# Eight norms' roots taken with tokens on the partitions, and spread by a product with diagonals

## What is computed

```
def rms_norm(x, g):
    y = x * rsqrt(mean(x * x, axis=-1) + EPS)
    return y * g

def modulate(h, shift, scale):
    return h * (1.0 + scale) + shift

h = modulate(rms_norm(x, norm_g[layer, 0]), sh, sc)
x = x + 0.5 * (1.0 + g) * swiglu(h, w_in, w_out)
...
x = x + gate * _rmsnorm(merged @ w_out, g_post)
```

## Time and profile before

| | us |
|---|---|
| median of three runs | 1347.66 |
| profiled execution | 1349.85 |
| span of its instructions | 1348.1 |
| TensorE with work | 1275.7 |
| VectorE busy | 1079.7 |
| ScalarE busy | 633.5 |
| GpSimd busy | 184.8 |

### The profile page before, as it was taken

How to read it: one execution, slowest core, us unless ns; L and a number is a source line. 1 busy time by engine, 2 the same in 40 slices (tenths; PEclk the granted TensorE clock), 3 DMA queues, 4 the chain that set the end, 5 groups by cost and what they waited for, 6 DMA issues and landing times.

```text
span 1348.1 us, 26718 instructions
## 1 busy us (share of the span) xinstructions
PE 1275.7 (95%) x10588; PEld 1238.6 (92%) x10588; DVE 1079.7 (80%) x1692; ACT 633.5 (47%) x990; POOL 184.8 (14%) x205
## 2 busy tenths in 40 slices
PE   1899999899999999999999999999999898999996
PEld 1899999799999889999999999999998788999996
DVE  6898977898877868889888686999876786895574
ACT  3543444444334556544457543433455465355452
POOL 4498900000000000000001000000001220430000
PEclk9899999999999999999999999999999998999998
DMA  9999897399897369988843468996656486455551
GB/s 362 341 326 308 305 311 262 126 309 333 303 314 272 125 216 358 335 301 303 310 138 113 156 247 300 329 321 207 229 165 169 88 146 151 158 166 180 178 181 48
DMA packets 110893, 319.82 MB, mean 237 GB/s; under 512 B 24096, under 2 KB 35648, under 8 KB 110528
## 3 DMA queue, kind: packets, MB, share of 16 engines
q1 hardware_dynamic: 110784, 318.31, 70.7%
HBM read 313.26 MB, written 5.01 MB: 236 GB/s over the span
## 4 chain that ended last, share of the span: by engine, by line
PE 85%; DVE 7%; ACT 3%; DMA 3%; issue 2%; SPq 1%; DVEq 0%; ACTq 0%
PE tiles L375 17%; PE tiles L377 17%; PE tiles L376 17%; PE acc L375 8%; PE acc L376 8%; PE acc L377 8%; PE nrm L547 1%; ACT w_hi L363 1%; DMA cons<-in_cons 1%; DVE w_lo L367 1%; PE tiles L573 1%; PE acc L686 1%; PE tiles L575 1%; PE tiles L590 1%; DVE arena L1456 1%
## 5 line engine op out<-in xcount | busy, mean ns | idle before, releaser
L363 ACT CAST w_hi<-land 128x1024 fp32r<-128x1024 f32 x391 | 408.3, 1047 | 465.7 <-PE tiles L377 289.1
L367 DVE TENSOR_TENSOR w_lo<-land,w_hi 128x1024 fp32r<-128x1024 f32 x391 | 484.9, 1247 | 160.2 <-ACT w_hi L363 159.3
L375 PE MATMUL tiles<-x_hi,w_hi 128*128 128x256 f32 x1384 | 395.2, 286 | 8.1 <-ACT arena L1133 3.9
L376 PE MATMUL tiles<-x_lo,w_hi 128*128 128x256 f32 x1384 | 392.6, 284 | 0.0
L377 PE MATMUL tiles<-x_hi,w_lo 128*128 128x256 f32 x1384 | 392.6, 284 | 0.0
L375 PEld LDWEIGHTS tiles<-x_hi,w_hi 128*128 128x128 f32 x1384 | 266.5, 193 | 11.2 <-ACT arena L1133 4.4
L376 PEld LDWEIGHTS tiles<-x_lo,w_hi 128*128 128x128 f32 x1384 | 266.5, 193 | 0.1
L377 PEld LDWEIGHTS tiles<-x_hi,w_lo 128*128 128x128 f32 x1384 | 266.4, 193 | 0.0
L1411 DVE SCALAR_TENSOR_TENSOR arena<-arena 128x1024 f32<-128x1024 f32 x184 | 227.1, 1237 | 12.3 <-ACT arena L1156 8.8
L375 PE MATMUL acc<-h_hi,w_hi 128*128 128x256 f32 x704 | 199.4, 283 | 1.5 <-DVE h_lo L1430 1.5
L376 PE MATMUL acc<-h_lo,w_hi 128*128 128x256 f32 x704 | 199.2, 283 | 0.0
(11 more groups left out here) (342 smaller groups left out, 1634.8 us busy)
## 6 DMA issues: line engine op xcount, KB each, us to landing
land<-in_stream SPq DMA_DIRECT2D x391, 512.0 KB, 4.5
arena<-in_gstream SPq DMA_DIRECT2D x184, 512.0 KB, 6.4
w_dram<-arena SPq DMA_DIRECT2D x3, 512.0 KB, 6.4
arena<-w_dram SPq DMA_DIRECT2D x6, 256.0 KB, 9.3
arena<-in_c_rows SPq DMA_DIRECT2D x2, 512.0 KB, 6.4
x<-in_x_t SPq DMA_DIRECT2D x1, 1024.0 KB, 12.9
arena<-in_ssm_bn SPq DMA_DIRECT2D x1, 1024.0 KB, 7.6
u_dram<-arena SPq DMA_DIRECT2D x1, 1024.0 KB, 5.3
```

Of the source, the lines that this page charges most:

```text
L363: nc.scalar.copy(w_hi[:, u % RING], land[:, u % LAND]).then_inc(hi_done, 1)
L367: nc.vector.tensor_tensor(w_lo[:, u % RING], land[:, u % LAND], w_hi[:, u % RING].bitcast(F32), ALU.subtract).then_inc(lo_done, 1)
L375: nc.tensor.matmul(outs, lh, rh, start=first, stop=False, **kw)
L376: nc.tensor.matmul(outs, lh, rl, start=False, stop=False, **kw)
```

## The change

The sums of squares, the roots and the reciprocals of all eight norms are taken with tokens on the partitions. `sum_squares` uses each squared tile as the loaded operand, in two halves of 128 tokens, with one column of ones streaming (`token_sums`): sixteen products of one column instead of eight of 256, into the last two columns of the bank `nrm`. Sqrt and reciprocal then have 128x2 values (`token_root`). VectorE multiplies the identity matrix with each of the two columns, which gives two diagonal matrices side by side (`root_diag`, 128x256, in the place where `rx` was), and signals `diag_done`. TensorE multiplies a matrix of ones with them (`spread_roots`), which puts the reciprocal root of every token on all partitions, and `rx` is now the first half of the bank `nrm` in PSUM. VectorE waits for that (`spread`) before it takes the normalised tiles. `keep_busy(7)` becomes `keep_busy(2)`, `spread_roots`, `keep_busy(3)`; at norm 6 `keep_busy(3)` becomes `keep_busy(2)`, `spread_roots`, `keep_busy(1)`, ahead of the small products; at norm 4 the spread stands behind two thirds of the transposes. Since the bank is now read until the last normalised tile, TensorE waits for `t_done` instead of `rt_done` before it writes there again.

```
+        eps_root, token_root = sb("eps_root", [P, 1])[:], sb("token_root", [P, 2])[:]
...
-        rx = region(36, [T])
+        root_diag = region(36, [2, P])
...
+        rx, sums = nrm[:, 0:T], nrm[:, 510:512]
...
                 if n:
-                    pe.wait_ge(rt_done, n)
+                    pe.wait_ge(t_done, KT * (n if n < 4 else n + 1))
                 for k in range(KT):
                     pe.wait_ge(sq_done, KT * n + k + 1)
-                    m = nc.tensor.matmul(nrm[:, 0:T], ones, t_buf[:, k], start=(k == 0), stop=(k == KT - 1))
+                    m = token_sums(t_buf[:, k], k == 0, k == KT - 1)
                 m.then_inc(nrm_done, 1)
+
+            def token_sums(squares, start, stop):
+                for tt in range(2):
+                    m = nc.tensor.matmul(sums[:, tt:tt + 1], squares[:, tt * P:(tt + 1) * P], ones[:, 0:1],
+                                         start=(start and tt == 0), stop=stop, skip_group_check=True)
+                return m
+
+            def spread_roots(n):
+
+                pe.wait_ge(diag_done, n + 1)
+                nc.tensor.matmul(rx, ones, root_diag.rearrange("p a b -> p (a b)"), start=True,
+                                 stop=True).then_inc(rx_done, 1)
...
             sum_squares(0)
+            spread_roots(0)
...
             sum_squares(1)
-            keep_busy(7)
+            keep_busy(2)
+            spread_roots(1)
+            keep_busy(3)
...
             for c, bank in enumerate((tiles[:, 0], tiles[:, 1], av_bank)):
                 turn_keys(c + 1, bank)
+                if c == 1:
+                    spread_roots(4)
             keep_busy(2)
...
             sum_squares(6)
-            keep_busy(3)
+            keep_busy(2)
+            spread_roots(6)
+            keep_busy(1)
...
             pe.wait_ge(sq_sum, KT - 2)
-            nc.tensor.matmul(nrm[:, 0:T], ones, t_buf[:, 0], start=True, stop=False)
+            token_sums(t_buf[:, 0], True, False)
             pe.wait_ge(sq_done, KT * 8)
-            nc.tensor.matmul(nrm[:, 0:T], ones, t_buf[:, KT - 1], start=False, stop=True).then_inc(nrm_done, 1)
+            token_sums(t_buf[:, KT - 1], False, True).then_inc(nrm_done, 1)
+            spread_roots(7)
...
-                nc.scalar.activation(rx, nrm[:, 0:T], ACT.Sqrt, bias=con("eps", 1), scale=1.0 / D).then_inc(rt_done, 1)
+                nc.scalar.activation(token_root, sums, ACT.Sqrt, bias=con("eps", 1), scale=1.0 / D).then_inc(rt_done, 1)
...
             def root(n):
                 dve.wait_ge(rt_done, n + 1)
-                link(V.reciprocal(rx, rx))
+                link(V.reciprocal(token_root, token_root))
+                V.tensor_tensor(root_diag, ident.unsqueeze(1).to_broadcast([P, 2, P]),
+                                token_root.unsqueeze(2).to_broadcast([P, 2, P]), ALU.mult).then_inc(diag_done, 1)
+
+            def spread(n):
+                dve.wait_ge(rx_done, n + 1)
```

More of the change, by code:

```diff
@@ L167, in build_program @@
         mods = sb("mods", [P, N_MOD])
-        eps_root = sb("eps_root", [P, 1])[:]
+        eps_root, token_root = sb("eps_root", [P, 1])[:], sb("token_root", [P, 2])[:]
         att_s = sb("att_s", [P, 2, 16])
@@ L287, in build_program @@
         sq_done, nrm_done, rt_done = sem("sq_done"), sem("nrm_done"), sem("rt_done")
+        diag_done, rx_done = sem("diag_done"), sem("rx_done")
         t_done, xh_done, xl_done = sem("t_done"), sem("xh_done"), sem("xl_done")
@@ L756, in _ @@
             sum_squares(2)
-            keep_busy(7)
+            keep_busy(2)
+            spread_roots(2)
+            keep_busy(3)
             ffn(1, 2)
             sum_squares(3)
-            keep_busy(7)
+            keep_busy(2)
+            spread_roots(3)
+            keep_busy(3)
             for part, bank_done in enumerate((v_bank, k_bank)):
@@ L778, in _ @@
             pe.wait_ge(base_done, 1)
-            pe.wait_ge(rt_done, 4)
+            pe.wait_ge(t_done, KT * 5)
             for r, s in ((0, 18), (1, 11)):
@@ L885, in _ @@
             sum_squares(5)
-            keep_busy(7)
+            keep_busy(2)
+            spread_roots(5)
+            keep_busy(3)
             ffn(3, 6)
             sum_squares(6)
-            keep_busy(3)
+            keep_busy(2)
+            spread_roots(6)
+            keep_busy(1)
             def lag_step(f):
@@ L1028, in _ @@
                 column_unit(UNIT["out"] + n, TILE["out"] + n, a_hi, a_lo)
-            pe.wait_ge(rt_done, 7)
+            pe.wait_ge(t_done, KT * N_STAGES)
             pe.wait_ge(sq_sum, KT - 2)
-            nc.tensor.matmul(nrm[:, 0:T], ones, t_buf[:, 0], start=True, stop=False)
+            token_sums(t_buf[:, 0], True, False)
             pe.wait_ge(sq_done, KT * 8)
-            nc.tensor.matmul(nrm[:, 0:T], ones, t_buf[:, KT - 1], start=False, stop=True).then_inc(nrm_done, 1)
+            token_sums(t_buf[:, KT - 1], False, True).then_inc(nrm_done, 1)
+            spread_roots(7)
         @block.scalar
@@ L1578, in _ @@
             norm_coef(0)
+            spread(0)
             for k in range(KT):
@@ L1598, in _ @@
             root(1)
+            spread(1)
             norm_t(1)
@@ L1610, in _ @@
             root(2)
+            spread(2)
             norm_t(2)
@@ L1615, in _ @@
             root(3)
+            spread(3)
             for k in range(KT):
@@ L1731, in _ @@
             root(4)
+            spread(4)
             norm_t(5)
@@ L1777, in _ @@
             root(5)
+            spread(5)
             norm_t(6)
@@ L1796, in _ @@
             root(6)
+            spread(6)
             norm_t(7)
@@ L1967, in _ @@
             root(7)
+            spread(7)
             for n, (a, b) in enumerate(LAST):
```

## The result

The changed kernel takes 1353.14 us (median of eight runs, 1351.45 to 1356.94) against 1347.62 (eight runs, 1346.59 to 1350.09): ratio 1.0048, 95% interval 1.004 to 1.0057. The forecast was 1344.2, a gain of 3.5 us; the kernel lost 5.5. Rival A, priced at 1351, is what happened. The profiled execution took 1353.46 us, its span 1351.7.

The account below looks back on a forecast made before the run. TensorE, with work in 95% of the span, plus its waits at the norms bound the kernel; 0.3 at norm 1, 2.9 at four norms, -0.35 at norm 6, 0.6 at the last sum to 3.5 us: 1344.2, range 1342.6 to 1354.

Parts of the forecast that it names:

- Rival A: One-column sums at the five inner norms let TensorE's clock fall to half, 1.4 us each, 7 in all: 1351; chance 0.38.
- C: Norm 1, ahead of the pooling: shorter TensorE idle time keeps the clock full, 1.4 us more gained: 1342.8; chance 0.08.
- the outer end of A's price: All five inner norms lose the clock during the sums, 4.1 us each, 20 in all: 1364.
- The sums: Sums of squares at the norms: 32 records take 3.57 us against 3.71, a gain of 0.13.
- Sqrt to spread: Between sums and normalised tiles: Sqrt, reciprocal, diagonal and spread take 1.68 us instead of 2.28, gain 0.60 a norm.
- PSUM reads: Normalised tiles reading one operand from PSUM: 476 ns against 478 in a like operation, so no cost.
- keep_busy just fits: Behind the sums: last three keep_busy products take 1.3 us, first x_hi tile comes 1.35 after the spread's issue; cost zero.
- B: Inner norms: slower diagonal and spread, and x_hi waiting for the third keep_busy product, cut the gain to 1.3: 1346.4; chance 0.10.
- Norm by norm: Gains: norm 1 0.3, four inner norms 0.73 each (2.9), norm 6 loses 0.35, last norm 0.6; sum 3.5 us.

Follow-up runs that it names:

- e1: The changed kernel with wide sums: each of the sixteen sum products streams 128 columns of ones instead of one; 1345.38 us.
- e6: Changed kernel with 128 streamed columns, norm 6's small products split around the spread, norm 1's reciprocal and diagonal earlier, nine keep_busy products behind norm 1's spread: 1342.24 us.

## Why the prediction was wrong

**The step that failed is the weighing of A.** The forecast's sum has no term for the clock: it puts at nothing what cost 7.8 us. The mechanism, its place and nearly its price stood in rival A: five falls at 1.4 each, 7 us; one column against 128 is 7.8. But it was put second, with 0.38 against 0.44. The argument that tipped it, "weight loads are still dense, one per record", is the one that the runs overturn: the loads left no gap (2.00 of 2.00 us) and the clock fell at norms 2 to 6 and during norm 1. The two rows without a fall (1.7 us of such sums among dense products, of which the prediction itself said that it proves little, and 1.3 us of idle time) were shorter than the 3.7 us of these sums, and the one longer row that it used, the 4.6 us of idle time at norm 1, spoke for A. The kernel before has two more such rows, which the prediction didn't use: TensorE's idle times of 4.36 us until 1056.33 and of 3.89 until 1125.80 go with a fall too. The wide range, 1342.6 to 1354, holds the measured time only because most of A was taken into it (its lower end calls C's time 1342.6, where C's own sum gives 1342.8).

That A's price comes so near is in part luck. Its 1.4 a fall was read from products at half clock; from first sum to first product, the changed kernel takes 0.8, 0.7, 1.0, 2.2 and 2.8 us longer than the wide one at norms 2 to 6. At norms 5 and 6, where the fall came during the sums, the first product started 1.7 and 3.5 us later than before: there the outer end of A's price shows.

**The sums.** 3.57 was predicted, 3.70 came at norm 3 (clock full until their end), so the gain of 0.13 is 0.01. The row of 0.107 us a record is of sums that wait for their squares once, ahead of the first; the pace here is a little slower, 0.11. What sets it wasn't tested.

**Sqrt to spread.** 1.68 predicted, 1.74 in e1 at norm 3, against 2.31 before. Sqrt 0.27 and diagonal 0.44 are right, reciprocal 0.18 for 0.16; the spread is 0.71 instead of 0.60, the value that stood in the earlier trace rows with "its wait in it" and was set aside. With 128 columns the norms 2 to 5 gain 0.46 or 0.47 each instead of 0.73.

**PSUM reads.** Free, as forecast (475 ns).

**keep_busy just fits.** At full clock it does. In e1 the chain runs through the keep_busy records behind the spread at norms 2, 4 and 5 (1.29, 0.86 and 1.30 us), but they delay nothing that can be measured: the first product starts 0.65 us after ScalarE began the first x_hi tile (norm 5: 776.07 to 776.72), as before (norm 6: 979.21 to 979.87). At norm 3 TensorE even stands idle for 0.43. So B's queue is refuted there, and of B only the longer spread is real. The fit itself was partly luck: on one side it left out the spread's own place in the queue (774.82 to 775.35 at norm 5), on the other it counted 0.4 for a spread that takes 0.71, and its 0.4, 0.49 and 0.52 are 1.41 and not 1.35. "At half clock they don't fit" is what the chain of norm 3 in the changed kernel shows.

**Norm by norm, at full clock.** Norm 1 gains 0.41 (0.3 forecast), norms 2 to 5 1.86 (2.9), norm 6 loses 0.68 (0.35; the queue was the right reason, the longer sums and spread the difference), and norm 7, from the end of the last product to the end of the first update of x, goes from 6.05 to 5.49, 0.56 (0.6). Together 2.15 instead of 3.5, and e1's median is 2.7 under its own runs of the kernel before. So with the clock kept the forecast would have been 1.2 us too low, and the rest, 7.8 us, is what one column costs against 128.

**C.** Refuted: in e1 the idle time ahead of the pooling products is 2.90 us, as C had it, and the clock falls all the same. In the changed kernel itself the fall at norm 1 came earlier, while TensorE had to wait for VectorE anyway, and the pooling products ran at full clock: from the first of them to the sums of norm 2 are 10.69 us, against 12.11 before and 12.17 in e1. So C's 1.4 us were gained there, but by accident and not for C's reason, and they hide a part of what A cost.

**What stays open.** What it is in the wider products that holds the clock can't be told from these runs, which changed the number of columns and, with it, the part of the bank that is written. Each kernel was traced once, so which norms lose the clock may differ between executions. Nor is it settled what a kept clock at norm 1 is worth in the whole time (e6), or why the same idle time around 1052 is followed by a shorter or a longer fall.

## What to carry to other kernels

A product that is shortened to one column may free no time (here one column took as long as 128, within 0.12 us in 3.8), and it can take away the clock of everything that follows: read the granted clock in windows of 2 us behind every stretch of thin products that a change makes, and let them stream more columns where that is free. When the nearest row on a risk is too short to bear it out, it is no evidence against it; look for the row of the same length. And filler work that stands in one queue with a real step, and just fits, is only filler while the clock is full.

## What the runs showed of the hardware

- TensorE's granted clock fell to half while its busy and load columns were full, behind 32 records that stream one column each in 3.7 us; with 64 or 128 columns a product, at nearly the same pace, it did not.
- A float32 product with 128 loaded columns costs nearly the same time whether one or 128 columns stream: 3.70 against 3.82 us for sixteen products.
- A fall at the same place of the program lasts 3.4 us in one kernel and 6.8 in another (around 1056: 3.4 before, 6.8 in the changed kernel), and the changed kernel, which has more falls, scatters more: 5.5 us from lowest to highest against 3.5. That the one is the reason for the other wasn't tested.
